# The first projection of a decoder trunk: input rows in places of their own, and two weight tiles times the first 528 tokens in plain fp32

## The reference

```
h = RMSNorm_pre(x)
layer 0: v, bg, cg, z = split(h @ W_in);  u = cg * v;  conv = causal conv of width 3 over u
         y = (bg * conv * silu(z)) @ W_out
layer 1: q, f, i, z = split(h @ W_in);  S_t = diag(f_t) S_(t-1) + k_t^T v_t;  o_t = q_t S_t
         y = (RMSNorm(o) * silu(z)) @ W_out
x = x + RMSNorm_post(y)
```

## Time and profile before

| what | value |
|---|---|
| three runs | 1077.11, 1077.96, 1078.79 us |
| median | 1077.96 us |
| profiled execution | 1079.18 us |
| its span in the trace | 1077.5 us |
| PE / PE weight loads / DVE / ACT busy | 98% / 92% / 67% / 36% |
| mean granted PE clock | 0.995 |

### The profile page before, as it was taken

The page is one execution under the profiler, slowest core; times in us unless marked ns, Lnnn a source line. Parts: engine busy times, 40 slices in busy tenths (PEclk is TensorE's granted clock), DMA queues, the critical chain, the costliest instruction groups (busy, mean ns, idle before and its releaser), DMA issues.

```text
span 1077.5 us, 20495 instructions
## 1 busy us (share of the span) xinstructions
PE 1052.9 (98%) x8043; PEld 987.8 (92%) x8043; DVE 724.4 (67%) x1294; ACT 384.8 (36%) x730; POOL 38.6 (4%) x53
## 2 busy tenths in 40 slices
PE   6999999999999999999999999999999999979997
PEld 5999999999999888789999999999999999967885
DVE  7798677677677645655658595775859577575146
ACT  7443333333334433443243242414233241533123
POOL 1000000000000000000101010010101010010000
PEclk9999999999999999999999999999999999989999
DMA  7102121121121352122212211211221121121143
GB/s 231 33 20 79 42 77 39 39 78 39 39 78 58 115 181 99 64 64 59 60 42 60 60 41 58 60 40 41 58 61 41 56 61 58 42 79 59 47 174 123
DMA packets 93317, 74.30 MB, mean 69 GB/s; under 512 B 2519, under 2 KB 85528, under 8 KB 93274
## 3 DMA queue, kind: packets, MB, share of 16 engines
q1 hardware_dynamic: 75482, 64.80, 19.2%
q10 hardware_dynamic: 17792, 8.91, 2.8%
HBM read 60.26 MB, written 13.44 MB: 68 GB/s over the span
## 4 chain that ended last, share of the span: by engine, by line
PE 89%; DVE 7%; DMA 2%; issue 1%; ACT 1%; SPq 0%; DVEq 0%; ACTq 0%
PE bank L565 34%; PE bank L613 23%; PE bank L712 17%; PE bank L585 2%; PE bank L786 2%; PE bank L859 1%; PE bank L866 1%; PE bank L780 1%; PE bank L868 1%; DMA wraw<-in_w_in 1%; PE bank L816 1%; DMA arena<-in_x_prompt 1%; PE bank L727 1%; PE bank L693 1%; PE bank L689 1%
## 5 line engine op out<-in xcount | busy, mean ns | idle before, releaser
L565 PE MATMUL bank<-reg_a,wsplit 128*128 128x352 f32 x2304 | 388.5, 326 | 0.6 <-ACT arena L1236 0.6
L565 PEld LDWEIGHTS bank<-reg_a,wsplit 128*128 128x128 f32 x2304 | 367.8, 188 | 4.0 <-issue 2.4
L613 PE MATMUL bank<-reg_a,wsplit 128*128 128x264 f32 x1344 | 165.5, 284 | 0.0
L613 PEld LDWEIGHTS bank<-reg_a,wsplit 128*128 128x128 f32 x1344 | 164.1, 188 | 0.0
L613 PE MATMUL bank<-reg_b,w_ring 128*128 128x264 f32 x1008 | 125.0, 284 | 1.0 <-ACT arena L1091 1.0
L613 PEld LDWEIGHTS bank<-reg_b,w_ring 128*128 128x128 f32 x1008 | 123.3, 188 | 1.3 <-DVE arena L1545 1.0
L712 PE MATMUL bank<-reg_a,reg_b 128*128 128x512 f32 x288 | 71.3, 402 | 0.9 <-DVE reg_a L1426 0.9
L712 PE MATMUL bank<-reg_b,reg_a 128*128 128x512 f32 x288 | 68.7, 395 | 0.0
L712 PEld LDWEIGHTS bank<-reg_a,reg_b 128*128 128x128 f32 x288 | 55.0, 192 | 14.3 <-DVE reg_a L1426 1.3
L712 PEld LDWEIGHTS bank<-reg_b,reg_a 128*128 128x128 f32 x288 | 53.9, 188 | 12.6
L1614 DVE TENSOR_TENSOR arena<-arena,bank 128x264 f32<-128x264 f32 x84 | 34.8, 427 | 33.6 <-PE bank L613 32.4
(11 more groups left out here) (260 smaller groups left out, 1481.9 us busy)
## 6 DMA issues: line engine op xcount, KB each, us to landing
wraw<-in_w_in SPq DMA_DIRECT2D x64, 512.0 KB, 4.0
arena<-in_x_prompt SPq DMA_DIRECT2D x16, 512.0 KB, 3.6
wraw<-in_w_out SPq DMA_DIRECT2D x16, 512.0 KB, 3.3
x_scratch<-arena SPq DMA_DIRECT2D x8, 512.0 KB, 2.6
arena<-in_state_hgrn ACTq DMA_DIRECT2D x8, 512.0 KB, 3.9
out<-arena ACTq DMA_DIRECT2D x8, 512.0 KB, 3.0
arena<-x_scratch SPq DMA_DIRECT2D x8, 512.0 KB, 3.2
out<-arena SPq DMA_DIRECT2D x7, 512.0 KB, 2.9
```

The lines of the kernel that those rows point to most:

```text
L565: mm = nc.tensor.matmul(bank[b][:, 0:CH], w[wi][:, k, :], rhs[hi], start=(k == 0 and i == 0), stop=(k == KT - 1 and i == 2))
L613: mm = nc.tensor.matmul(bank[banks[q]][:, 0:QT], w[wi][:, k, :], B_OP[name][hi][:, k, q * QT:(q + 1) * QT], start=(start and k == 0 and i ...
```

## The change

- **Loads.** The eight full row tiles get places of their own in the upper part of `reg_a` (`x_rows_in`), the last tile has one more. SP issues them without waits, with the two weight tiles between them. The six small loads are issued by ACT, ahead of its first instruction.
- **Quarters.** Their bounds become 0, 256, 528, 768, 1056. They are split in the order 2, 3, 0, 1.
- **Plain products.** Tiles t = 0 and 1 times the tokens 0 to 527 are done out of `wraw` and `h_raw` in plain fp32, unsplit, one row tile at a time (`plain_rows(t, i)`, eight products of 128 or, for i = 3, 144 columns), between the turns. They take the place of groups 0 to 3. Groups 4 to 15 stay. Quarters 0 and 1 still have to be split for t = 2 and 3.
- **Fillers.** `keep_busy(15)` and `keep_busy(4)` stand before the first turn, those between the turns go.
- **Order on ACT and DVE.** DVE weighs tile i directly behind its scaling for tiles 0 to 5. `first_hi(2)`, `first_lo(2)` and `first_u(2)` stand in the opening; behind `first_lo(2)` comes `token_lo(1)`, then the small instructions, `first_u(3)` and t1. The copy of the conv state and one small subtraction come behind the first scaling.
- **Weights 2 and 3.** SP loads them into `wraw` once three and four groups are done, since the plain products read the raw tiles.

```diff
+QE = (0, 256, 528, 768, T)
+SPLIT_ORDER = (2, 3, 0, 1)
...
+        x_rows_in = nc.alloc_sbuf_tensor_at("x_rows_in", [P, CK * D], F32, offset=reg_b_at - 4 * 2 * SLOT)
...
+        def x_row(i):
+
+            return x_rows_in[:, i * D:(i + 1) * D] if i < CK else st_x
...
             load_input(0)
-
-            for src, row, n in ((norm_pre, PRE, 2), (norm_post, POST, 2), (conv_w[0], CW, 3), (lb_logits, LBL, 1)):
-                sp.dma_start(st_vec[row:row + n * KT, :], src.rearrange("l (k p) -> (l k) p", p=P)).then_inc(vec_in, 16)
-            sp.dma_start(st_vec[ONRM:ONRM + 1, :], onorm).then_inc(vec_in, 16)
-            sp.dma_start(st_row[0:2 * NB, :], state_conv[0].rearrange("b w c -> (b w) c")).then_inc(cst_in, 16)
-            for i in range(9):
-                if i >= 3:
-                    sp.wait_ge(S_DN.sem, S_DN.at(i - 3, "xn"))
-                if i:
-                    load_input(i)
-                if i == 3:
-                    load_w(0, wsrc(w_in[0], 0), 0, 0, False)
-                if i == 4:
-                    load_w(1, wsrc(w_in[0], 2 * D), 1, 0, False)
+            load_w(0, wsrc(w_in[0], 0), 0, 0, False)
+            load_input(1)
+            load_input(2)
+            load_w(1, wsrc(w_in[0], 2 * D), 1, 0, False)
+            for i in range(3, TT):
+                load_input(i)
 
             COL0 = (0, 2 * D, D, 3 * D)
             for t in (2, 3):
+                sp.wait_ge(proj_done, t + 1)
                 load_w(t, wsrc(w_in[0], COL0[t]), t % 2, 1)
...
+            def keep_busy(n):
+
+                for k in range(n):
+                    nc.tensor.transpose(bank[0][:, 0:P], ident[:, :], ident[:, :])
+
             pe.wait_ge(pool_ev.sem, pool_ev.at(0, "id"))
+            keep_busy(15)
...
-            pe.wait_ge(K_DVE, 2)
+            keep_busy(4)
 
             pairs = ((3, 4), (5, 6))
             def turn_input(i):
                 r = rows_of(i)
                 pe.wait_ge(S_DN.sem, S_DN.at(i, "xn"))
+                if i == 1:
+                    pe.wait_ge(K_DVE, 2)
...
-                pe.wait_ge(S_LO.sem, S_LO.at(q, "lo"))
+                pe.wait_ge(S_LO.sem, S_LO.at(SPLIT_ORDER.index(q), "lo"))
                 w = slot(t % 2)
-                cols = slice(q % 2 * QT, (q % 2 + 1) * QT)
+                cols = slice(QE[q] - q // 2 * HT, QE[q + 1] - q // 2 * HT)
...
-            BETWEEN = {2: 12, 3: 8, 4: 8}
-            START = {4: 0, 5: 1, 6: 2, 7: 3, 8: 4}
-            for i in range(TT):
-                turn_input(i)
-                if i in BETWEEN:
-                    keep_busy(BETWEEN[i])
-                if i in START:
-                    first_group(START[i])
+            def plain_rows(t, i):
+
+                q = i // 2
+                b = J0_BANK[2 * q + t]
+                first, end = i * P, QE[q + 1] if i % 2 else (i + 1) * P
+                if i % 2 == 0:
+                    pe.wait_ge(bank_free[2 * q + t], emptied(0))
+                pe.wait_ge(w_in_s[t], 16)
+                pe.wait_ge(S_DT.sem, S_DT.at((end - 1) // P, "tb"))
+                for k in range(KT):
+                    mm = nc.tensor.matmul(bank[b][:, first - QE[q]:end - QE[q]], wraw[:, t, k, :], h_raw[:, k, first:end],
+                                          start=(k == 0), stop=(k == KT - 1))
+                if i % 2:
+                    mm.then_inc(proj_done, 1)
+
+            turn_input(0)
+            plain_rows(0, 0)
+            turn_input(1)
+            plain_rows(0, 1)
+            turn_input(2)
+            plain_rows(1, 0)
+            turn_input(3)
+            plain_rows(1, 1)
+            turn_input(4)
+            plain_rows(0, 2)
+            turn_input(5)
+            plain_rows(1, 2)
+            plain_rows(0, 3)
+            turn_input(6)
+            plain_rows(1, 3)
+            turn_input(7)
+            first_group(4)
+            turn_input(8)
...
+            for src, row, n in ((norm_pre, PRE, 2), (norm_post, POST, 2), (conv_w[0], CW, 3), (lb_logits, LBL, 1)):
+                act.dma_start(st_vec[row:row + n * KT, :], src.rearrange("l (k p) -> (l k) p", p=P)).then_inc(vec_in, 16)
+            act.dma_start(st_vec[ONRM:ONRM + 1, :], onorm).then_inc(vec_in, 16)
+            act.dma_start(st_row[0:2 * NB, :], state_conv[0].rearrange("b w c -> (b w) c")).then_inc(cst_in, 16)
             act.wait_ge(eps_set, 1)
             A(small[:, 47:48], eps[:, :], ACT.Sqrt)
-            normalise(0)
-            normalise(1)
-            for i in range(9):
-                if i + 2 < TT:
-                    normalise(i + 2)
-                if i == 1:
-                    first_hi(0)
-                if i == 3:
-                    first_hi(1)
-                if i in (2, 4, 6, 8):
-                    token_hi(i // 2 - 1)
-                if i == 6:
-                    first_v(0)
-                if i == 8:
-                    first_v(1)
+            for i in range(6):
+                normalise(i)
+            first_hi(0)
+            first_v(0)
+            normalise(6)
+            first_hi(1)
+            token_hi(2)
+            normalise(7)
+            normalise(8)
+            first_v(1)
+            token_hi(3)
+            token_hi(0)
+            first_v(2)
+            token_hi(1)
+            first_hi(2)
+            first_v(3)
             act.wait_ge(K_DVE, 3)
             A(st_lb[:, 1], st_lb[:, 0], ACT.Exp).then_inc(K_ACT, 1)
-            first_v(2)
-            first_v(3)
...
-            first_hi(2)
...
-            dve.wait_ge(K_PE, 2)
-            V.tensor_copy(c_st, bank[6][:, 0:KT * 16]).then_inc(K_DVE, 1)
-
-            dve.wait_ge(K_DVE, 2)
-            V.tensor_tensor(st_lb[:, 0], cst[:, LBL:LBL + KT], cst[:, LBL:LBL + KT], ALU.subtract).then_inc(K_DVE, 1)
...
-            normalise(0)
-            for i in range(9):
-                r = P if i < 8 else NSAMP
-                if i < 8:
-                    normalise(i + 1)
+            def weigh(i):
+
+                r = rows_of(i)
                 for half, name in enumerate(("ta", "tb")):
                     dve.wait_ge(S_PE.sem, S_PE.at(i, name))
                     src = bank[((3, 4), (5, 6))[i % 2][half]][:, :].rearrange("p (k t) -> p k t", k=4)[:, :, 0:r]
                     g = cst[:, PRE + 4 * half:PRE + 4 * half + 4].unsqueeze(2).broadcast_to([P, 4, r])
                     V.tensor_tensor(h_raw[:, 4 * half:4 * half + 4, i * P:i * P + r], src, g, ALU.mult).then_inc(S_DT.now(name), 1)
-                if i in (2, 4):
-                    first_lo(i // 2 - 1)
-                if i in (3, 5, 7):
-                    token_lo(i // 2 - 1)
-                if i == 8:
-                    first_u(0)
+
+            normalise(0)
+            dve.wait_ge(K_PE, 2)
+            V.tensor_copy(c_st, bank[6][:, 0:KT * 16]).then_inc(K_DVE, 1)
+            dve.wait_ge(K_DVE, 2)
+            V.tensor_tensor(st_lb[:, 0], cst[:, LBL:LBL + KT], cst[:, LBL:LBL + KT], ALU.subtract).then_inc(K_DVE, 1)
+            weigh(0)
+            for i in range(1, 6):
+                normalise(i)
+                weigh(i)
+            normalise(6)
+            first_lo(0)
+            first_u(0)
+            token_lo(2)
+            weigh(6)
+            normalise(7)
+            first_lo(1)
+            weigh(7)
+            normalise(8)
+            weigh(8)
             token_lo(3)
             first_u(1)
+            first_u(2)
+            token_lo(0)
+            first_lo(2)
+            token_lo(1)
...
-            first_lo(2)
-            first_u(2)
```

More of the change, by code:

```diff
@@ L155, in build @@
         st_vec = pl.take(P)
-        st_x = [pl.take(D) for _ in range(3)]
+        st_x = pl.take(D)
         st_n = [pl.take(D) for _ in range(2)]
@@ L240, in build @@
         x1_dram = nc.dram_tensor("x1_scratch", (T, D), F32, kind="Internal").ap()
-        x_in = [sem(f"x_in{i}") for i in range(3)]
+        x_in = [sem(f"x_in{i}") for i in range(TT)]
         vec_in, cst_in = sem("vec_in"), sem("cst_in")
@@ L584, in first_group @@
                     for i, (wi, hi) in enumerate(((0, 0), (1, 0), (0, 1))):
-                        mm = nc.tensor.matmul(bank[b][:, 0:QT], w[wi][:, k, :], src[hi][:, k % KH, cols],
+                        mm = nc.tensor.matmul(bank[b][:, 0:QE[q + 1] - QE[q]], w[wi][:, k, :], src[hi][:, k % KH, cols],
                                               start=(k == 0 and i == 0), stop=(k == KT - 1 and i == 2))
                 mm.then_inc(proj_done, 1)
-            def keep_busy(n):
-                for k in range(n):
-                    nc.tensor.transpose(bank[0][:, 0:P], ident[:, :], ident[:, :])
-            BETWEEN = {2: 12, 3: 8, 4: 8}
-            START = {4: 0, 5: 1, 6: 2, 7: 3, 8: 4}
-            for i in range(TT):
-                turn_input(i)
-                if i in BETWEEN:
-                    keep_busy(BETWEEN[i])
-                if i in START:
-                    first_group(START[i])
+            def plain_rows(t, i):
[29 more added lines that the diff above has]
```

(15 more changed lines are left out.)

25 lines of the change are left out of this document (12 added, 13 removed).

## The result

| | before | after |
|---|---|---|
| median (four executions each, same chip) | 1077.53 us | 1088.16 us (1087.52 to 1088.75) |
| ratio, 95% interval | | 1.0098 [1.0084, 1.0112] |
| profiled execution, its span | 1079.18, 1077.5 us | 1088.75, 1087.0 us |
| mean granted PE clock | 0.995 | 0.990 |

The change costs 10.6 us. The forecast was 1081.0, some 3 us slower, with a range up to 1084.6.

The account below looks back on a forecast made before the run. DVE's chain from t1 with its weight loads was taken to bound 48 to 104 us, PE afterwards. Terms 0, -3.1, +3.0, -0.4, +2.5, +1.2, -0.2 gave +3.0: 1081.0 us, range 1076.8 to 1084.6 (8 in 10).

Parts of the forecast that it names:

- Part 1: Opening loads: row tiles in own places, SP without waits, small loads on ACT; cost nothing, first turn at 7.3 us.
- The rival: Opening: small loads through ACT land late behind 512 KB ones, first turn at 8.5 us, total 1082.2; chance 0.04.
- The order of the loads: Opening: SP's load issues hidden behind DVE and PE work; without that cover, second tile late by at most 1 us.
- The clock: PE's clock falls in new waits, losing 1.7 to 3 us, or the slow opening costs 2.2 more; chance 0.25.
- the walk: Opening stepped through: first turn 7.3 us, turn 2 at 14.9, group 4 at 33.0, t1 at 51.4.
- The wait ahead of group 6: PE stands from 38.9 to 41.6 us because first_group(6) needs token_lo(3): 2.7 us.
- `token_lo(1)` and the small instructions ahead of t1: On DVE between first_lo(2) and t1: token_lo(1) adds 2.5 us, the small lower-bound and mask instructions 1.2 us.
- The wait ahead of group 12: PE ready at 59.9 us waits 2.1 us, until DVE frees the first bank about 62.0.
- The table load: ACT's opening: stands behind the six small loads, next ACTIVATE 1.3 us after its start; the skill's 2.66 us not followed.
- the 3.1 us that the walk gained up to group 4: PE starts first_group(4) at 33.0 instead of 36.06 us; given back by a 2.7 us wait and the wider group.
- The question for the change is when t1 starts: DVE's first token sum, at 48.42 us before, sets the stretch to 104 us; forecast at 51.4, 3.0 us late.
- PE's present 1.0 us of waiting there becomes about 1.4: PE's wait near 104 us, after DVE's chain and two load waits, grows from 1.0 to about 1.4 us.

Follow-up runs that it names:

- experiment 1: Changed kernel with the six small loads issued by SP behind the first row tile instead of by ACT; 1082.99 us against 1077.03 for the kernel before.
- experiment 2: Changed kernel, small loads still on ACT, but SP holds its further large loads until they have landed; 1085.93 us against 1078.00 for the kernel before.
- experiment 3: Kernel before with row tiles in own places, free-running SP, changed load order; small loads on SP 1080.46 us (ratio 1.0022), on ACT 1081.02 us (1.0041).
- experiment 4: Changed kernel with 45 fillers instead of 15 ahead of the first small transpose; 1086.62 us against 1077.03 for the kernel before.
- experiment 5: Changed kernel with 23 fillers between groups 5 and 6, run twice: 1089.53, then 1088.78 us beside the unaltered changed kernel's 1088.21.
- experiment 6: Changed kernel with token_lo(1) and small instructions ahead of first_lo(2) on DVE, exponential ahead of first_hi(2) on ACT; 1085.93 us against 1077.03 before.
- experiment 7: Kernel before with only t1 moved ahead of first_lo(2) on DVE; 1076.72 us against 1077.56, ratio 0.999.
- last kernel of 9: The first kernel of 9 with 24 and 2 fillers instead of 15 and 4; 1075.22 us against 1078.00 for the kernel before, ratio 0.9974.
- experiment 9: Changed kernel's plain products kept, small loads on SP, row tiles earlier, DVE's order laid out anew; two filler counts, 1077.05 and 1075.22 us.
- 8: Changed kernel with small loads on SP, second row tile ahead of weights, experiment 6's order and 23 fillers in PE's wait; 1079.44 us against 1077.56 before.
- first kernel of 9: Plain products kept, small loads on SP, row tiles earlier, DVE's order laid out anew, 15 and 4 fillers; 1077.05 us against 1077.56 for the kernel before.

## Why the prediction was wrong in size and right in sign

**The step that failed first** is in Part 1: "Cost nothing", with the small loads through ACT landing as they did from SP. The forecast reckoned with the time to issue them (2.5 us, right: 0.81 to 3.59) and not with the time to land. In the kernel before, the conv state takes 2.0 us from issue to landing; after, with five 512 KB loads of SP's issued ahead of it and more behind, 6.1 us. Experiments 1 and 2 show it: the vectors come 3.5 to 3.9 us earlier as soon as either they or the large loads are moved. The rival had the mechanism, and 0.04; it took 8.5 us for the first turn, and it was 11.2, so that it priced the mechanism at 1.2 us where it cost 3.9. The Trainium skill, DMA: Bandwidth & Descriptors, section Issuing engines are not separate DMA queues, says that a second issuing engine saves issue time alone, since all transfers interleave on the same 16 engines. The traces agree: 6.1 us to landing from ACT beside SP's loads, 2.4 us from ACT without them. That would have given the rival more.

**The order of the loads** was held to be hidden too, "if that cover were gone, the second tile would be first to be late, by at most the 1 us" between its normalisation and its turn. The second row tile stands behind a weight tile now. In experiment 3 this costs 2.5 us by itself. In the changed kernel no wait for the second row tile shows on PE, since the first tile is late as well; once it is not, the wait is there (1.52 us in experiment 1).

**The clock** was a rival of 0.25, with two places, "1.7 to 3 us" in a wait and "2.2 us more" at the start. Both came. Between the first turn and that of tile 2 the profile has 2.9 us more than the walk; the same stretch took 7.86 us at full speed (experiment 4) and 10.48 here, so 2.6 us are the clock and 0.3 the walk. Behind group 6 it has 1.8 us more, of which the fillers of experiment 5 take away 1.5. The failure is that the cases were taken as alternatives, each added to the forecast by itself and topped at 1084, with the late loads a third. They don't exclude one another, and in this kernel all came. Added up, 3.9 us for the small loads, 2.6 and 1.5 for the clock, and 0.9 in all for steps of the walk that were too short, they give the 8.9 us.

**What held.** From the turn of tile 2 to group 4 the walk gave 18.1 us, and it was 18.05. The wait ahead of group 6 was 2.5 for 2.7 us. `token_lo(1)` and the small instructions ahead of t1, priced at 3.7 us, cost 3.0 that moving them gives back (experiment 6). The wait ahead of group 12 is 2.3 for 2.1 us. The table load came behind the DMA issues, 1.30 us before the next ACTIVATE, as the row of before had it. And the 3.1 us that the walk gained up to group 4 were given back by the wait and the wider group, as it said.

**One reading was too simple.** "The question for the change is when t1 starts" holds where t1 is late, as in the changed kernel. It does not hold for an early one: DVE's chain from t1 also passes the gates, which wait for PE's groups, and in the kernel before DVE already waits 0.15 us for PE there. Experiment 7 moved t1 by 5.7 us and t2 not at all. The forecast's walk from t1 to 104 us left this meeting point out.

**One estimate had the wrong sign.** "PE's present 1.0 us of waiting there becomes about 1.4": it vanished. The second weight pair took 7.1 us from issue until ACT had it in the kernel before (80.95 to 88.11) and 6.0 us after (92.80 to 98.85), and with it went 1.1 of the 11.9 us. No experiment changed this load by itself. In experiments 1 and 7, in the repeat of the changed kernel and in the last kernel of 9 the same load took 5.9 to 6.1 us, so it is the 7.1 of before that stands apart, whatever the change does.

**What the change could have been worth.** The plain products are no loss in themselves: experiment 9 keeps them and is 2.8 us faster than before, though by how much they contribute to this, as against the order of the work and the loads, no run separates. That order without the plain products is an untested rival for the whole 2.8 us; t1 early alone gives 0.8 us at an interval that touches no change (experiment 7).

## What to carry to other kernels

A small load that gates the first instruction belongs ahead of the large ones; moved to an idle engine's queue it is issued sooner and lands later, so read the time to landing and not the time to issue. Where rivals don't exclude one another, the upper end of a range is their sum. Work moved into the stretch right ahead of the instruction that starts the next chain is paid for almost in full (3.0 of 3.7 us here), even if the engine is idle a few microseconds earlier: put it there instead. But follow the chain to where it next waits for another engine before you count on starting it earlier.

## What the hardware showed that was not expected

- **A small load beside bulk.** 64 KB of conv state: 2.0 us from issue to landing with SP issuing it behind one row tile, 6.1 us from ACT with the large loads running beside it.
- **The clock behind a wait.** After PE's wait of 2.5 us in the changed kernel the granted clock of the next 3.3 us was 0.50 in the first profile and 0.67 in the repeat. In all six profiles that had this wait without fillers, the 48 products behind it took 8.1 to 8.2 us instead of 6.6. After 1.65 us the clock did not fall. Behind the next wait, of 2.0 to 2.3 us, the 48 products took 6.1 us in all five profiles in which group 6 had been slow (granted clock 1.00 in the first), and 7.6 us in both in which fillers had kept it fast (0.77 and 0.78).
- **The start differs from one execution to the next.** The opening of the changed kernel was profiled five times (itself twice, experiment 5 twice, experiment 6): its first turn was slow each time, its first plain products four times of five. With the small vectors on time and 15 fillers, the first turn was fast in experiments 1 and 2 and slow in 8 and in the first kernel of 9, though PE had no wait of over 0.2 us ahead of it in either. The Trainium skill, TensorE: Matmul & The Clock Gate, Part 1, says that the number of slow matmuls at a kernel's start varies from run to run; the traces agree. With more fillers (experiment 4, last kernel of 9) both were fast in two profiles of two.
- **The granted clock of the opening isn't always what the spacing shows.** In the repeat of the changed kernel the profile gives 1.00 for 14.3 to 17.9 us, in which eight plain products took the same 3.75 us as at 0.50 in the first profile. The same stands in the first kernel of 9, from 10.2 to 13.7 us. In the opening the duration of a known group is the safer reading.
